# Two pairs of modulation rows: spread by matmul, or stored outside and loaded onto every partition

## What is computed

```python
mod_l = jnp.split((jax.nn.silu(c) @ ada_w[l] + ada_b[l])[:, None, :], 6, axis=-1)
mod_c = jnp.split((jax.nn.silu(c_ctx) @ ada_w[l] + ada_b[l])[None, None, :], 6, axis=-1)
h = _modulate(_rmsnorm(x, norm1_g[l]), mod_l[0], mod_l[1])      # h * (1 + scale) + shift
hc = _modulate(_rmsnorm(xc, norm1_g[l]), mod_c[0], mod_c[1])
```

## Time and profile before

| | |
|---|---|
| median of 3 runs | 814.26 us (814.02 to 815.16) |
| the profiled execution | 813.56 us, of which the span of the trace is 812.3 us |
| mean granted clock of TensorE | 0.998 |
| TensorE, matmuls | 799.7 us busy, 98% |
| TensorE, weight loads | 685.6 us busy, 84% |
| VectorE | 627.7 us busy, 77% |
| ScalarE | 474.9 us busy, 58% |
| GpSimd | 41.5 us busy, 5% |
| transfers | 160.05 MB, mean 197 GB/s |

### The profile page before, as it was taken

The page is one execution under the profiler, slowest core; times in us unless marked ns, Lnnn a source line. Parts: engine busy times, 40 slices in busy tenths (PEclk is TensorE's granted clock), DMA queues, the critical chain, the costliest instruction groups (busy, mean ns, idle before and its releaser), DMA issues.

```text
span 812.3 us, 12701 instructions
## 1 busy us (share of the span) xinstructions
PE 799.7 (98%) x5059; PEld 685.6 (84%) x5059; DVE 627.7 (77%) x939; ACT 474.9 (58%) x811; POOL 41.5 (5%) x52
## 2 busy tenths in 40 slices
PE   8999999999999999999999999999999999999996
PEld 5999998878988999999987789985576888888885
DVE  6785687646799889799795885998849877767775
ACT  6564444446587868868946552647636655455443
POOL 7010003600000000000000000000000000000000
PEclk9999999999999999999999999999999999999999
DMA  8977897784634443456346772936637565555631
GB/s 290 318 263 232 251 275 223 248 293 137 204 119 141 148 143 128 153 157 207 126 162 227 284 245 94 372 125 232 214 131 249 192 197 169 204 187 178 206 104 52
DMA packets 105701, 160.05 MB, mean 197 GB/s; under 512 B 11317, under 2 KB 74137, under 8 KB 103338
## 3 DMA queue, kind: packets, MB, share of 16 engines
q1 hardware_dynamic: 105354, 158.71, 59.3%
q10 hardware_dynamic: 288, 0.52, 0.2%
HBM read 156.02 MB, written 3.21 MB: 196 GB/s over the span
## 4 chain that ended last, share of the span: by engine, by line
PE 91%; DVE 5%; ACT 2%; DMA 1%; issue 1%; SPq 0%; ACTq 0%; DVEq 0%
PE acc L472 10%; PE acc L474 9%; PE acc L473 9%; PE acc L493 9%; PE acc L524 8%; PE acc L526 8%; PE acc L525 8%; PE acc L494 4%; PE misc L1325 3%; PE misc L2337 3%; PE misc L2339 2%; PE misc L2338 2%; PE misc L923 2%; PE acc L497 1%; DVE w_lo L445 1%; PE misc L650 1%
## 5 line engine op out<-in xcount | busy, mean ns | idle before, releaser
L445 DVE TENSOR_TENSOR w_lo<-raw,w_hi 128x2048 fp32r<-128x2048 f32 x113 | 260.9, 2320 | 56.6 <-ACT w_hi L438 56.3
L438 ACT ACTIVATE w_hi<-raw 128x2048 fp32r<-128x2048 f32 x113 | 215.8, 1912 | 61.1 <-PE acc L526 17.0
L472 PE MATMUL acc<-X,w_hi 128*128 128x256 f32 x592 | 168.9, 285 | 0.0
L474 PE MATMUL acc<-X,w_lo 128*128 128x256 f32 x592 | 167.5, 283 | 0.0
L473 PE MATMUL acc<-X,w_hi 128*128 128x256 f32 x592 | 167.4, 283 | 0.0
L472 PEld LDWEIGHTS acc<-X,w_hi 128*128 128x128 f32 x592 | 113.5, 192 | 4.6 <-issue 3.4
L473 PEld LDWEIGHTS acc<-X,w_hi 128*128 128x128 f32 x592 | 113.5, 192 | 0.3
L474 PEld LDWEIGHTS acc<-X,w_lo 128*128 128x128 f32 x592 | 113.5, 192 | 0.0
L493 PE MATMUL acc<-X,w_hi 128*128 128x512 f32 x308 | 110.3, 397 | 0.0
L494 PE MATMUL acc<-X,w_lo 128*128 128x256 f32 x308 | 86.4, 280 | 0.0
L524 PE MATMUL acc<-w_hi,X 128*128 128x512 f32 (+1 forms) x176 | 68.9, 392 | 0.7 <-DVE w_lo L415 0.5
(11 more groups left out here) (304 smaller groups left out, 1495.2 us busy)
## 6 DMA issues: line engine op xcount, KB each, us to landing
raw<-in_hgrn_w_in_dram SPq DMA_DIRECT2D x32, 1024.0 KB, 5.7
ada_raw<-in_ada_w_dram SPq DMA_DIRECT2D x24, 1024.0 KB, 7.1
raw<-in_ffn_w_up_dram SPq DMA_DIRECT2D x22, 1024.0 KB, 5.1
raw<-in_pool_w_in_dram SPq DMA_DIRECT2D x15, 1024.0 KB, 6.3
raw<-in_ffn_w_down_dram SPq DMA_DIRECT2D x11, 1024.0 KB, 5.0
raw<-in_w_in_dram SPq DMA_DIRECT2D x10, 1024.0 KB, 6.4
raw<-in_pool_w_out_dram SPq DMA_DIRECT2D x8, 1024.0 KB, 5.4
raw<-in_hgrn_w_out_dram SPq DMA_DIRECT2D x8, 1024.0 KB, 5.2
```

Source lines behind the costliest of these rows:

```text
L438: self.hi_done.up(act.activation(self.w_hi[v % RING][:, 0:w], self.raw[j][:, 0:w], ACT.Copy), v)
L445: self.lo_done.up(dve.tensor_tensor(self.w_lo[j][:, 0:w], self.raw[j][:, 0:w], self.w_hi[v % RING][:, 0:w].bitcast(F32), ALU.subtract), v)
L472: pe.matmul(o, wh[:, k, c:c + P], xh[:, k, :], start=k == 0, stop=False)
L474: m = pe.matmul(o, wl[:, k, c:c + P], xh[:, k, :], start=False, stop=k == K - 1)
```

## The change

The context's and the second block's shift and scale are no longer spread by TensorE. SP stores the eight quarters from `ada` into a tensor in device memory, `rows_dram`, right after it has issued the context's loads, and after the scores of the last heads loads each of the four rows back onto all partitions, with g loaded once into a tile of its own. The gain is made by one instruction of 1024 columns from SBUF (`dve_gain_row`), the shifts need no copy. The calls of `pe_rows` and `act_shift_rows` of this stage go, and with them their waits; TensorE does its half of unit 66 ahead of the waits for the heads and the gain; VectorE makes the context's gain behind the low parts of the heads instead of ahead of the split of unit 67. `dve_gain_rows` stays for the feed-forward part.

```diff
--- before.py
+++ after.py
@@ -192,6 +192,7 @@
         self.f_row = at(36, "f_row", [D])
         self.J = at(32, "J", [D])
         self.JF = at(56, "JF", [2, D])
+        self.n_gain = at(40, "n_gain", [D])
         self.c_gain = at(56, "c_gain", [D])
         self.c_shift = at(60, "c_shift", [D])
         self.c_tok = at(90, "c_tok", [2, D])
@@ -236,6 +237,7 @@
         self.Y = at(46, "Y", [2, D])
         self.OT = at(16, "OT", [2, D])
         self.scratch = nc.dram_tensor("rpb_padded", (NA_HEADS * 15, P), F32, kind="Internal").ap()
+        self.rows_dram = nc.dram_tensor("modulation_rows", (2, 2 * D), F32, kind="Internal").ap()
         self.bias_dram = nc.dram_tensor("bias", (P, 2 * NA_HEADS * TOK), F32, kind="Internal").ap()
 
         bank = self.stack.enter_context
@@ -262,7 +264,7 @@
 
         self.x_in = [signal(f"x_in{n}") for n in range(2)]
         self.par_in = signal("parameters_in")
-        self.gain_in = {n: signal(f"gain_in_{n}") for n in ("first", "out", "ctx", "final", "in2", "ffn", "end")}
+        self.gain_in = {n: signal(f"gain_in_{n}") for n in ("first", "out", "norm", "final", "ffn", "end")}
         self.ada_in = [signal(f"ada_in{n}") for n in range(8)]
         self.ctx_in = [signal(f"context_in{n}") for n in range(2)]
         self.ada_b_in = signal("ada_bias_in")
@@ -273,6 +275,9 @@
         self.scr_out = signal("scratch_out")
         self.bias_in = signal("bias_in")
         self.bias_out = signal("bias_out")
+
+        self.rows_out = signal("rows_out")
+        self.rows_back = {n: signal(f"rows_back_{n}") for n in ("ctx_gain", "ctx_shift", "in2_gain", "in2_shift")}
         self.bias_back = signal("bias_back")
         self.stored = signal("out_stored")
 
@@ -904,8 +909,6 @@
         pe, n = self.nc.tensor, self.ada_at(a)
         if a == 0:
             pe.wait_ge(self.A.h, self.A["silu_c"])
-        if a == KD:
-            pe.wait_ge(self.A.h, self.A["shift", "in2"])
         if a == 2 * KD:
             pe.wait_ge(self.V.h, self.V["ada", 1])
         if a == 2 * KD + 4:
@@ -1611,12 +1614,21 @@
         sp.wait_ge(self.T.h, self.T["ada", KD - 1])
         for half in range(2):
             self.ctx_in[half].up(sp.dma_start(self.c_tok[:, half, :], c[:, half, :]), "ctx", by=16)
+        sp.wait_ge(self.V.h, self.V["ada", 0])
+        for m in range(2):
+            for j in range(4):
+                self.rows_out.up(sp.dma_start(self.rows_dram[m:m + 1, j * 512:j * 512 + 512],
+                                              self.ada[32 * j + m:32 * j + m + 1, 0, :]), "all", by=16)
         self.sp_stream(self.first(self.u_hgrn_out), self.first(self.u_k))
 
         sp.wait_ge(self.T.h, self.T["scored", PAIRS - 1, 1])
-        self.gain_in["ctx"].up(sp.dma_start(self.c_gain[:, :], self.spread("norm1_g_2", 0, D, P)), "all", by=16)
+        sp.wait_ge(self.rows_out.h, self.rows_out["all"])
+        self.gain_in["norm"].up(sp.dma_start(self.n_gain[:, :], self.spread("norm1_g_2", 0, D, P)), "all", by=16)
+        for name, row, m, c in (("ctx_gain", self.c_gain, 1, 1), ("ctx_shift", self.c_shift, 1, 0),
+                                ("in2_gain", self.x_gain, 0, 1), ("in2_shift", self.x_shift, 0, 0)):
+            src = bass.AP(self.rows_dram.tensor, (2 * m + c) * D, [[0, P], [1, D]])
+            self.rows_back[name].up(sp.dma_start(row[:, :], src), "all", by=16)
         self.gain_in["final"].up(sp.dma_start(self.f_row[:, :], self.spread("final_g", 0, D, P)), "all", by=16)
-        self.gain_in["in2"].up(sp.dma_start(self.x_gain[:, :], self.spread("norm1_g_2", 0, D, P)), "all", by=16)
         self.ws_in_s.up(sp.dma_start(self.ws_in[:, :, :], h["sg_w_2"][0].rearrange("g p q -> p g q")), "all", by=16)
         k = self.first(self.u_k)
         self.sp_stream(k, k + 2)
@@ -1646,22 +1658,16 @@
         self.pe_out1_part(0, 2)
         self.pe_values_of(last)
         self.pe_out1_part(1, 0)
-        pe.wait_ge(self.A.h, self.A["exact", last, 1])
-        self.pe_rows("ctx_gain", 0, 1, (2, 3), (0, 1))
         self.pe_out1_part(1, 1)
         self.pe_turn_heads(3, 0)
         self.pe_turn_heads(3, 1)
-        pe.wait_ge(self.V.h, self.V["gain", "ctx"])
-        self.pe_rows("ctx_shift", 0, 1, (0, 1), (0, 1))
         self.pe_out1_part(1, 2)
+        self.pe_out1_part(0, 3, (0,))
+
+        pe.wait_ge(self.A.h, self.A["exact", last, 1])
         for r in range(2):
             pe.wait_ge(self.V.h, self.V["mb_lo", 3, r])
-        self.pe_rows("in2_gain", 0, 0, (2, 3), (2, 3))
-        pe.wait_ge(self.A.h, self.A["shift", "ctx"])
-        self.pe_rows("in2_shift", 0, 0, (0, 1), (0, 1))
-        self.pe_out1_part(0, 3, (0,))
         pe.wait_ge(self.V.h, self.V["gain", "in2"])
-        pe.wait_ge(self.A.h, self.A["shift", "in2"])
         for half in range(2):
             for c in range(2):
                 self.pe_turn("ctx", half, c, self.c_tok)
@@ -1670,11 +1676,15 @@
             self.pe_out1_part(c, 3, (1,))
         pe.wait_ge(self.V.h, self.V["xl", "ctx", 1, 1])
 
-    def act_shift_rows(self, name, row, bank=0):
-        act = self.nc.scalar
-        act.wait_ge(self.T.h, self.T["rows", name + "_shift"])
-        for c in range(2):
-            self.A.up(act.activation(row[:, c * 512:c * 512 + 512], self.misc[bank + c][:, :], ACT.Copy), "shift", name)
+    def dve_gain_row(self, name, row):
+
+        dve = self.nc.vector
+        dve.wait_ge(self.gain_in["norm"].h, self.gain_in["norm"]["all"])
+        dve.wait_ge(self.rows_back[name + "_gain"].h, self.rows_back[name + "_gain"]["all"])
+        n = self.V.up(dve.scalar_tensor_tensor(out=row[:, :], in0=row[:, :], scalar=1.0, in1=self.n_gain[:, :],
+                                               op0=ALU.add, op1=ALU.mult), "gain", name)
+        dve.wait_ge(self.V.h, n)
+        dve.wait_ge(self.rows_back[name + "_shift"].h, self.rows_back[name + "_shift"]["all"])
 
     def dve_gain_rows(self, name, row, bank):
         dve = self.nc.vector
@@ -1702,9 +1712,7 @@
         self.hi(self.first(u0 + 1, 0) + RING)
         self.act_heads_high(3, 0)
         self.act_heads_high(3, 1)
-        self.act_shift_rows("ctx", self.c_shift)
         self.hi(self.first(u0 + 1, 1) + RING)
-        self.act_shift_rows("in2", self.x_shift)
         self.hi(self.first(u0 + 1, 2) + RING)
         for half in range(2):
             for c in range(2):
@@ -1753,15 +1761,14 @@
         self.dve_scores_of(last, 1)
         self.lo(self.first(u0, 2) + RING)
         self.dve_gate_of(last)
-        self.dve_gain_rows("ctx", self.c_gain, 0)
         self.lo(self.first(u0 + 1, 0) + RING)
         self.dve_heads_low(3, 0)
         self.dve_heads_low(3, 1)
-        dve.wait_ge(self.A.h, self.A["shift", "ctx"])
+        self.dve_gain_row("ctx", self.c_gain)
         for half in range(2):
             self.dve_root("ctx", half)
             self.dve_scale("ctx", half, self.c_tok, self.c_tok, self.c_gain, self.c_shift)
-        self.dve_gain_rows("in2", self.x_gain, 2)
+        self.dve_gain_row("in2", self.x_gain)
         self.lo(self.first(u0 + 1, 1) + RING)
         self.add_out(u0, 0, 0)
         for half in range(2):
@@ -1776,7 +1783,6 @@
         self.dve_part("final", 1)
         self.add_out(u0 + 1, 1, 1)
 
-        dve.wait_ge(self.A.h, self.A["shift", "in2"])
         dve.wait_ge(self.tile_done.h, self.tiles_of[u0 + 1][1][0])
         self.dve_root("in2", 0)
         self.dve_scale("in2", 0, self.x_tok, self.XN2, self.x_gain, self.x_shift)
@@ -1960,7 +1966,7 @@
         caf = self.CA[:, :, :].rearrange("p f t -> p (f t)")
         dve.wait_ge(self.A.h, self.A["square", "in2", 1, 0])
         z = V.up(dve.memset(self.CP[:, :, :], 0.0))
-        dve.wait_ge(self.T.h, self.T["rows", "in2_shift"])
+        dve.wait_ge(self.rows_out.h, self.rows_out["all"])
         V.up(dve.memset(self.ada[:, 0, :], 0.0), "ada_cleared_again")
         for f in range(2):
             self.wait_freed(dve, cv, 2 + f)
```

## The result

The changed kernel takes 816.38 us in the median of 17 runs (813.36 to 818.59), the kernel before 814.15 in the median of 17 beside it (813.38 to 815.16). The ratio is 1.0024, with a 95% interval of 1.0017 to 1.0030: slower, by a little over what can be told from no change. The forecast was 813.8 us, in a range up to 816.2. The profiled execution took 817.32 us, of which 816.0 is the span.

A forecast was written before the change was run, and what follows sets the result against it. TensorE, busy 98% of the span, was taken as the bound; of 3.62 us removed, 3.16 become waiting for VectorE. 813.56 - 0.46 = 813.10 us profiled, 813.8 by the median; 8-in-10 range 812.4 to 816.2.

The forecast's parts named there:

- TensorE's part: Broadcast matmuls removed at three places in TensorE's stream: 1.27 + 1.06 + 1.29 = 3.62 us goes.
- the second place: Second broadcast place, behind transposes: 1.06 us goes from TensorE. In the rival's bullet instead: the stretch at 509 to 521 us.
- VectorE's part: Context's gain now behind the heads' low parts, 1.22 us; second gain ends at 455.67, so TensorE waits 3.16 us.
- The step from VectorE's end to the transposes: Handover before the context's transposes: 0.10 us to the next engine plus 0.08 for the weight load; transposes start at 455.85.
- What is late next is VectorE's gain of the second block: At TensorE's wait before the context's transposes: nothing queued behind it can go ahead, leaving 0.46 of 3.62 us.
- ScalarE, SP and the transfers: Four shift copies gone, eight stores at 0.49 us each, three more 512 KB loads: cost nothing, transfer bounds 0 to +1.5 us.
- The clock: TensorE's granted clock around the new hole, forecast to stay at 1.00 through 450 to 465: nothing taken in the sum.
- The rival: The clock falls in TensorE's new hole before the context's transposes; chance 0.14.
- a first price of the clock: The clock rival's smaller cost, 1.75 us, giving 815.6; taken in by the range up to 816.2.
- an upper one: The clock rival's larger cost, twice the first price, giving 817.3; left out of the range.

The follow-up runs named there:

- filled: The changed kernel with 14 small matmuls, results unused, put into TensorE's new hole ahead of the wait for the second block's gain: 812.56 us.
- half filled: The changed kernel with 7 small matmuls instead of 14 at the start of TensorE's new hole, leaving 1.53 us of it: 813.12 us.
- the kernel with a hole of 2.02 us: The changed kernel, but VectorE makes the context's gain where it stood before, ahead of the split of unit 67: 814.12 us; second profile 814.25 us.
- the kernel before with a hole: The kernel before with three gain-sized VectorE instructions, results unused, ahead of the second block's gain, and nothing of the change: 818.77 us.

## Why the prediction was wrong

- **TensorE's part, right.** 3.62 us were counted as going. With no hole behind them, 3.81 went; the second place was counted 0.2 too low.
- **VectorE's part, right.** The hole of 3.16 us was 3.28; the gain instructions took 1.21 and 1.22 for 1.22. The step from VectorE's end to the transposes, taken as 0.10 and 0.08 by choice, was 0.26 (456.54 to 456.80; the weight load of the transposes starts at 456.77). What was left at full clock, 0.46 by the sum, is 0.50 in the stage of the two filled kernels. "What is late next is VectorE's gain of the second block" is right for the kernel as written, but the sum took that wait as given, where the code no longer needs it.
- **ScalarE, SP and the transfers, right.** Priced at nothing, and the kernel before with these transfers has a ratio to itself of 0.9999 (0.9990 to 1.0008). The stores were cheaper than taken, 0.31 us each for 0.49.
- **The clock, wrong.** This is the step that failed: "I take nothing in the sum." The term for the clock was put at nothing; it measured 1.80 and 2.82 us in the two profiles of the changed kernel. One row of before, the end of the trace, shows a fall some 3.5 us after the last matmul's record (the window view has 0.84 in the mean of 809 to 810, and 0.50 behind it), and I read it as the least that it takes. It was one sample: at the ends of the ten traces of this case the fall comes 2.6 us (filled) to 4.4 us (half filled) after the last matmul's record. In the changed kernel the clock fell 2.0 us after the last matmul in one profile, and in the other just after the hole, 0.8 us into the transposes; in the kernel with a hole of 2.02 us it fell as the transposes began, 2.07 us after the last matmul's record (452.45 + 0.40 to 454.92); in the kernel before with a hole, 2.73 us after it (456.23 + 0.40 to 459.36). Of 18 runs with a hole of 3.3 us, 16 lost the clock, going by their mean clock; of 12 with 2.0 us, 7; of 11 with 1.5 us none. I had also taken the eight slow records at the very start for transposes at the lower level, and they don't show that: by line 877 they are plain matmuls, at 2.07 / 8 = 0.26 us each where the same instruction takes 3.29 / 28 = 0.12 in the filled hole, the window view has the clock at 1.00 from 0 to 9 us, and what makes them slow was not shown. That the lower level, 0.50 in the window view, doubles the time is shown by the sixteen transposes, 1.91 and 3.64 us.
- **The rival, right in kind and half right in size.** The range takes in a first price of the clock and leaves out an upper one. They were my estimates: half of 3.5 us, the time from the last matmul to the fall at the end of the trace, is 1.75 us, which gives 815.6, and twice that gives 817.3. No run shows these terms themselves. What the runs showed in their place is 3.4 us at half clock in three profiles and 6.8 us in the fourth (455.52 to 462.36), and in the stage of the changed kernel a loss of 1.80 and 2.82 us. Its two profiled executions took 815.52 and 817.32, and that the second agrees so well is luck: its trace was 0.82 us late before the stage began, and lost 0.58 at the second place. The rival's chance was put at 0.14, and 15 of 17 runs went its way. The four profiles that have a fall show one order: TensorE waits for 2.0 to 3.3 us, the clock falls to 0.50 in that wait or within 0.8 us behind it, and it is back at 1.00 between 3.0 and 5.6 us after TensorE has started again. They don't say which hole is long enough: two other profiles, with holes of 1.53 and 2.02 us, kept the full clock. I gave the single row more weight than one sample can bear.
- **The range.** Its upper end, 816.2, took in the first price and left out the upper one; the median is 816.38.
- What would have helped: the sum itself said that 3.16 of 3.62 us turn into a wait. A forecast that has most of a gain end in a hole of TensorE has to price the clock first, or ask why the gain instruction isn't left in the idle time where it was.

## What to carry to other kernels

Taking work from an engine that is the bound only pays as far as the next engine is ahead of it: here TensorE gave 3.6 us, and VectorE, with half a microsecond in hand and a gain of 1.21 us put on its path, took back 3.1. A hole in TensorE can cost more than its length: holes of 2.0 and 3.3 us lost the clock in 7 of 12 and 16 of 18 runs here, at 1.5 to 2.8 us in the four profiles that have a fall, so price it before anything else. When a value moves from PSUM to SBUF, look for waits that guarded its bank. When work moves to another engine, put it in that engine's idle time and check that its operands have landed by then; moving two instructions into such time was worth 5.9 us here.

## What was not expected of the hardware

- Fourteen matmuls whose result nobody reads, put into the hole, made the kernel 3.8 us faster (816.38 to 812.56).
- The same kernel with the same hole of 2.02 us kept the clock in 5 of 12 runs and lost it in 7, and the two groups lie 1.5 us apart with no run between (812.58 and 814.12).
- A median over runs can hide such a thing: the kernel with the context's gain early has a median of 814.12, though five of its eleven runs are about 1.8 us faster.
- The wait from the last matmul to the fall of the clock isn't the same from run to run: 2.0 and 4.1 us (452.78 to 456.88) in two profiles of one kernel with one hole, 2.6 to 4.4 us at the ends of the ten traces.
